# First norm, first chunk and last norm of a two-layer hybrid decoder trunk

## The reference

```python
def rmsnorm(x, g):
    y = xf * lax.rsqrt(jnp.mean(xf * xf, axis=-1, keepdims=True) + EPS)
    return y * g
for l in range(DEPTH):
    x = x + 0.5 * swiglu_ffn(rmsnorm(x, norm_ffn1[l]), w_ffn1_in[l], w_ffn1_out[l])
    u = rmsnorm(x, norm_mix[l]); proj = u @ w_in[l]
    ...  # retention, pooling and convolution branches, gated and merged
    x = x + merged @ w_out[l]
    x = x + 0.5 * swiglu_ffn(rmsnorm(x, norm_ffn2[l]), w_ffn2_in[l], w_ffn2_out[l])
return rmsnorm(x, norm_final)
```

## Time and profile before

| | us |
|---|---|
| median of 3 runs | 1225.2 (1223.81 to 1225.21) |
| the profiled execution: its own time | 1225.4 |
| the profiled execution: span in the trace | 1223.6 |
| PE busy in the span | 1176.9 (96%) |
| DVE busy | 755.6 (62%) |
| ACT busy | 533.9 (44%) |
| POOL busy | 56.6 (5%) |
| mean granted clock of PE, share of full | 0.988 |

### The profile page before, as it was taken

One profiled execution on the slowest core, in us unless ns is written; L12 is line 12 of the kernel. 1 busy time (PEld: TensorE's weight loads), 2 busy tenths in 40 slices (PEclk: granted clock), 3 DMA queues, 4 the chain that ended last, 5 costly groups with the idle time before them and its releaser, 6 DMA issues.

```text
span 1223.6 us, 13278 instructions
## 1 busy us (share of the span) xinstructions
PE 1176.9 (96%) x5360; PEld 969.5 (79%) x5360; DVE 755.6 (62%) x903; ACT 533.9 (44%) x586; POOL 56.6 (5%) x73
## 2 busy tenths in 40 slices
PE   6999999999988999999999999999999699999997
PEld 5888887888866878888878888878887587888886
DVE  5554465796798664554465545467959977645442
ACT  7444345443434454443364444354433255444331
POOL 3000001000000010000020000020000001000000
PEclk9999999999988999999999999999999899999999
DMA  8655364553643455445554545545346344644440
GB/s 331 241 202 189 123 243 167 207 180 111 225 155 137 143 202 184 165 167 206 206 209 170 207 149 211 192 170 206 121 143 253 121 157 153 224 175 170 171 172 35
DMA packets 33661, 220.02 MB, mean 180 GB/s; under 512 B 3760, under 2 KB 4144, under 8 KB 8640
## 3 DMA queue, kind: packets, MB, share of 16 engines
q1 hardware_dynamic: 31104, 212.09, 47.4%
q0 software_dynamic: 1648, 6.06, 1.4%
q10 hardware_dynamic: 848, 1.02, 0.2%
HBM read 218.10 MB, written 1.05 MB: 179 GB/s over the span
## 4 chain that ended last, share of the span: by engine, by line
PE 86%; DVE 10%; ACT 2%; DMA 1%; issue 1%; SPq 0%; DVEq 0%; POOL 0%; POOLq 0%; ACTq 0%
PE acc L302 27%; PE acc L304 27%; PE acc L303 27%; DVE w_lo L884 4%; DVE y L1064 4%; PE tr L360 4%; DMA raw<-in_weights 1%; ACT w_hi L599 1%; DVE xT_lo L918 1%; ACT xT_hi L611 0%; DVE gates L1132 0%; DVE ua L1113 0%; DVE x L898 0%; PE tr L451 0%; PE tr L461 0%
## 5 line engine op out<-in xcount | busy, mean ns | idle before, releaser
L884 DVE TENSOR_TENSOR w_lo<-raw,w_hi 128x2048 fp32r<-128x2048 f32 (+2 forms) x207 | 451.1, 2212 | 108.4 <-ACT w_hi L599 107.8
L599 ACT CAST w_hi<-raw 128x2048 fp32r<-128x2048 f32 (+2 forms) x207 | 380.2, 1850 | 254.8 <-PE acc L304 252.9
L302 PE MATMUL acc<-w_hi,xT_hi 128*128 128x512 f32 x1184 | 475.8, 402 | 13.3 <-DVE gates L1132 6.3
L304 PE MATMUL acc<-w_hi,xT_lo 128*128 128x512 f32 x1184 | 465.6, 393 | 0.0
L303 PE MATMUL acc<-w_lo,xT_hi 128*128 128x512 f32 x1184 | 464.9, 393 | 0.0
L302 PEld LDWEIGHTS acc<-w_hi,xT_hi 128*128 128x128 f32 x1184 | 225.0, 190 | 59.6 <-DVE gates L1132 7.1
L304 PEld LDWEIGHTS acc<-w_hi,xT_lo 128*128 128x128 f32 x1184 | 224.4, 190 | 48.8
L303 PEld LDWEIGHTS acc<-w_lo,xT_hi 128*128 128x128 f32 x1184 | 224.9, 190 | 43.6
L937 DVE SCALAR_TENSOR_TENSOR h<-acc,rs,silu_gate 128x256 f32<-128x256 f32 x88 | 42.5, 483 | 223.0 <-ACT silu_gate L643 223.0
L302 PE MATMUL acc<-w_hi,hT_hi 128*128 128x512 f32 x352 | 137.9, 392 | 0.0
L304 PE MATMUL acc<-w_hi,hT_lo 128*128 128x512 f32 x352 | 137.1, 389 | 0.0
(11 more groups left out here) (104 smaller groups left out, 556.1 us busy)
## 6 DMA issues: line engine op xcount, KB each, us to landing
raw<-in_weights SPq DMA_DIRECT2D x195, 1024.0 KB, 4.8
raw<-in_weights SPq DMA_DIRECT2D x8, 512.0 KB, 3.4
bias<-in_gate_bias POOLq DMA_DIRECT2D x6, 512.0 KB, 7.7
raw<-in_weights SPq DMA_DIRECT2D x8, 256.0 KB, 3.6
scale_row<-in_pool_scale POOLq DMA_DIRECT2D x2, 512.0 KB, 9.1
out<-x SPq DMA_DIRECT2D x4, 256.0 KB, 2.1
x<-in_x ACTq DMA_DIRECT2D x3, 256.0 KB, 7.6
band<-in_band POOLq DMA_DIRECT2D x1, 768.0 KB, 8.8
```

Source lines behind the costliest of these rows:

```text
L302: nc.tensor.matmul(o, a_hi, b_hi, start=first, stop=False)
L304: return nc.tensor.matmul(o, a_lo, b_hi, start=False, stop=last)
L599: nc.scalar.copy(w_hi[:, hf % HIGHS, 0:n], raw[:, hf % RAWS, 0:n]).then_inc(hi_split, 1)
L884: nc.vector.tensor_tensor(w_lo[:, hf % RAWS, 0:n], raw[:, hf % RAWS, 0:n], w_hi[:, hf % HIGHS, 0:n].bitcast(F32), ALU.subtract).then_inc(l ...
```

## The change

- The array `ident` gets 8 more columns that hold the gains of the first norm; `x_high` and `x_low` of the first norm read their scale there, and ACT and DVE wait for `ident_landed` in place of `par_landed`. The load of `par` is issued after the two quarters of x for t = 1, and is waited for at the end of the first FFN.
- Before and between PE's first transposes, 7, 2 and 6 matmuls of zeros run (`keep_busy`), on a row that DVE sets at the start (`warm_set`). They write to a bank of PSUM (`ret`) that nobody reads then.
- `cast_first` and `sub_first` now go over eight eighths of chunk 0: half 1 is cast and subtracted in four quarters too (its load is one DMA as before), and PE waits at each k for its eighth.
- `x_high` and `x_low` of t = 1 come right behind the eighths. The squares of t = 0, `cast(2)` and `cast(3)` come behind `x_high` of t = 1, and `sub(2)` behind `x_low` of t = 1.
- The end: the squares are made by halves (n = 0, 1), POOL adds eps to the first, adds the second, and takes the power (two instructions behind the last squares); DVE multiplies each half by the gain as soon as it is added (`weighted`); behind the root, ACT scales and stores half 0, DVE scales and SP stores half 1.
- POOL's load of `scale_row` of layer 0 waits for the first product.

```diff
-        ident = sb("ident", [P, P])
+        ident_gain = sb("ident_gain", [P, P + KT])
+        ident = ident_gain[:, 0:P]
...
-                    if t == 0 and hf == 0:
+                    if t == 0 and hf < 2 and k < KT - 1:
                         pe.wait_ge(first_lo, k + 1)
+                    elif t == 0 and hf == 1:
+                        pe.wait_ge(lo_split, 1)
...
+            def keep_busy(n):
+                warm = scale_row[:].bitcast(BF16)
+                for _ in range(n):
+                    nc.tensor.matmul(ret[:, 0, :], warm[:, 0:P], warm[:, 0:NB], start=True, stop=True)
+            pe.wait_ge(warm_set, 1)
+            keep_busy(7)
             pe.wait_ge(ident_landed, 16)
             turn_x(0, 0, 0, 0)
+            keep_busy(2)
             turn_x(0, 0, 0, 1)
+            keep_busy(6)
...
-            act.dma_start(par[:], params.rearrange("l p n -> p l n")).then_inc(par_landed, 16)
             for c in (0, 1):
                 act.dma_start(x[:, 1, columns(c)], x_part(1, c)).then_inc(x_landed[1][c], 16)
+            act.dma_start(par[:], params.rearrange("l p n -> p l n")).then_inc(par_landed, 16)
...
             def cast_first(i):
-                act.wait_ge(first_landed[i], 16)
-                nc.scalar.copy(w_hi[:, 0, columns(i)], raw[:, 0, columns(i)]).then_inc(first_hi, 1)
+                hf, s = i // 4, columns(i % 4)
+                if i < 4:
+                    act.wait_ge(first_landed[i], 16)
+                elif i == 4:
+                    act.wait_ge(raw_landed[1], 16)
+                nc.scalar.copy(w_hi[:, hf, s], raw[:, hf, s]
+                               ).then_inc(first_hi if i < 7 else hi_split, 1)
...
                 x_high(l, norm, 1, 0)
                 x_high(l, norm, 1, 1)
+                if l == 0 and norm == 0:
+                    square(l, norm, 0)
+                    for hf in (2, 3):
+                        cast(hf)
                 cast(l * HALVES + 2 * g + 4)
...
-            act.wait_ge(par_landed, 16)
+            act.wait_ge(ident_landed, 16)
             x_high(0, 0, 0, 0)
             cast_first(0)
+            cast_first(1)
             x_high(0, 0, 0, 1)
-            for i in range(1, 4):
+            for i in range(2, 8):
                 cast_first(i)
-            cast(1)
-            square(0, 0, 0)
-            cast(2)
-            cast(3)
...
+            for t in range(T):
+                for n in (0, 1):
+                    wait_acc_taken(act, L - 1, FFN2 + FB, t, n)
+                    nc.scalar.activation(squares[:, columns(n)], x[:, t, columns(n)], ACT.Square,
+                                         scale=D ** -0.5, accum_out=end_meansq[:, t, n:n + 1]
+                                         ).then_inc(end_meansq_ready, 1)
+                act.wait_ge(end_rs_ready, t + 1)
+                act.wait_ge(end_weighted, 2 * t + 1)
+                nc.scalar.activation(weighted[:, t, columns(0)], weighted[:, t, columns(0)],
+                                     ACT.Copy, scale=end_rs[:, t:t + 1]).then_inc(out_ready[0], 1)
+                act.wait_ge(out_ready[0], t + 1)
+                act.dma_start(out.rearrange("a (t p) d -> p (a t) d", p=P)[:, t, columns(0)],
+                              weighted[:, t, columns(0)]).then_inc(stored, 16)
...
+            nc.vector.memset(scale_row[:, 0:NB // 2], 0.0).then_inc(warm_set, 1)
...
             for t in range(T):
                 for n in (0, 1):
                     add_next(L, 0, t, n)
-            dve.wait_ge(bias_landed, 48 * L + 16)
-            for t in range(T):
-                dve.wait_ge(rs_ready, 6 * L + t + 1)
-                for n in (0, 1):
                     wait_acc_taken(dve, L - 1, FFN2 + FB, t, n)
-                    nc.vector.scalar_tensor_tensor(x[:, t, columns(n)], x[:, t, columns(n)],
-                                                   rs[:, t:t + 1], bias[:, columns(n)],
-                                                   ALU.mult, ALU.mult).then_inc(out_ready, 1)
+                    nc.vector.tensor_tensor(weighted[:, t, columns(n)], x[:, t, columns(n)],
+                                            bias[:, columns(n)], ALU.mult
+                                            ).then_inc(end_weighted, 1)
+                dve.wait_ge(end_weighted, 2 * t + 2)
+                dve.wait_ge(end_rs_ready, t + 1)
+                nc.vector.tensor_scalar(weighted[:, t, columns(1)], weighted[:, t, columns(1)],
+                                        end_rs[:, t:t + 1], None, ALU.mult
+                                        ).then_inc(out_ready[1], 1)
```

More of the change, by code:

```diff
@@ L177, in trunk @@
         rot = st
+        weighted = gates
         ysilu = v
@@ L233, in trunk @@
         setup_act = sem("setup_act")
-        out_ready = sem("out_ready")
+        warm_set = sem("warm_set")
+        end_meansq_ready = sem("end_meansq_ready")
+        end_eps_added = sem("end_eps_added")
+        end_totalled = sem("end_totalled")
+        end_rs_ready = sem("end_rs_ready")
+        end_weighted = sem("end_weighted")
+        out_ready = [sem(f"out_ready{n}") for n in (0, 1)]
         PRODUCT = {}
@@ L243, in trunk, with gain @@
         uses = [[0, 0] for _ in range(T)]
+        def gain(l, norm, k):
+            if l == 0 and norm == 0:
+                return ident_gain[:, P + k:P + k + 1]
+            return par[:, l, PAR_GAIN[norm] + k:PAR_GAIN[norm] + k + 1]
         def tokens(t):
@@ L609, in x_high @@
                     k = 4 * c + i
-                    col = PAR_GAIN[norm] + k
                     nc.scalar.activation(xT_hi[:, k, tokens(t)],
                                          bank(("x", l, norm, t, c))[:, i * P:(i + 1) * P],
-                                         ACT.Copy, scale=par[:, l, col:col + 1]
+                                         ACT.Copy, scale=gain(l, norm, k)
                                          ).then_inc(x_hi_ready, 1)
@@ L888, in sub_first @@
             def sub_first(i):
[L889 to L892, removed]
+                hf, s = i // 4, columns(i % 4)
+                if i < 7:
+                    dve.wait_ge(first_hi, i + 1)
+                else:
+                    dve.wait_ge(hi_split, 1)
+                nc.vector.tensor_tensor(w_lo[:, hf, s], raw[:, hf, s], w_hi[:, hf, s].bitcast(F32),
+                                        ALU.subtract).then_inc(first_lo if i < 7 else lo_split, 1)
             def add_x(l, g, use, t, n, half):
@@ L916, in x_low @@
                     k = 4 * c + i
-                    col = PAR_GAIN[norm] + k
                     a = nc.vector.scalar_tensor_tensor(
                         xT_lo[:, k, tokens(t)], bank(name)[:, i * P:(i + 1) * P],
-                        par[:, l, col:col + 1], xT_hi[:, k, tokens(t)].bitcast(F32),
+                        gain(l, norm, k), xT_hi[:, k, tokens(t)].bitcast(F32),
                         ALU.mult, ALU.subtract)
@@ L961, in ffn @@
                         begin(l, 3 * f)
+                        if l == f == 0:
+                            sub(2)
                     else:
@@ L1289, in mixer @@
                 finish(l, 3, l * HALVES + 2 * (M_OUT + 1) + 4)
-            dve.wait_ge(par_landed, 16)
+            dve.wait_ge(ident_landed, 16)
             x_low(0, 0, 0, 0)
             sub_first(0)
+            sub_first(1)
             x_low(0, 0, 0, 1)
-            for i in range(1, 4):
+            for i in range(2, 8):
                 sub_first(i)
-            sub(1)
-            sub(2)
             for l in range(L):
@@ L1387, in _ @@
                            ).then_inc(bias_landed, 16)
-            norm_factor(L, 0)
+            for t in range(T):
+                s = slice(t, t + 1)
+                pool.wait_ge(end_meansq_ready, 2 * t + 1)
+                nc.gpsimd.tensor_tensor(end_eps[:, s], end_meansq[:, t, 0:1], small[:, 1:2],
+                                        ALU.add).then_inc(end_eps_added, 1)
+                pool.wait_ge(end_eps_added, t + 1)
+                pool.wait_ge(end_meansq_ready, 2 * t + 2)
+                nc.gpsimd.tensor_tensor(end_total[:, s], end_meansq[:, t, 1:2], end_eps[:, s],
+                                        ALU.add).then_inc(end_totalled, 1)
+                pool.wait_ge(end_totalled, t + 1)
+                nc.gpsimd.tensor_tensor(end_rs[:, s], end_total[:, s], small[:, 0:1],
+                                        ALU.pow).then_inc(end_rs_ready, 1)
 def decay_table():
```

28 lines of the change are left out of this document (19 added, 9 removed).

## The result

| | median, us | runs | ratio to before, 95% interval |
|---|---|---|---|
| before | 1224.75 | 4 (1223.81 to 1225.21) | |
| changed | 1239.54 | 4 (1238.88 to 1240.61) | 1.0122, 1.0109 to 1.0134 |

The changed kernel is 14.8 us slower; the forecast was 1221.4, faster. (The median before is of four executions here, of three where it stood at 1225.2.) The profiled execution took 1238.9 us with a span of 1236.7.

What follows compares the result with a forecast made beforehand. PE, working 96% of the span, was taken as the bound, with gains only at the two ends: 1225.4 - 2.7 (start) - 1.1 (end) = 1221.6, forecast 1221.4 because the profiled execution lies 0.2 us above the median; range 1219.0 to 1223.3.

Steps and rivals of the forecast that it cites:

- rival D: Rings and hidden values move some tens of bytes; if reads slow, all 5360 matmuls pay: 1232 us at 2 ns; chance 0.03.
- Gains with the identity: Start: ACT can begin before 8.45 us; by itself no gain, since ACT waits for half 1 until 13.13.
- Products of zeros: Start of PE: seven end at 4.2 us, first transposes slip from 3.88 to 4.2, first product at 8.4 instead of 11.52.
- Rival B: Products of zeros fail, PE at 1.2 GHz through all of t = 0: gain 2.6 us, 1222.6; chance 0.12.
- rival A: Clock doesn't fall in the wait before k = 4: gain 4.0 + 1.1 = 5.1 us, 1220.1; chance 0.30.
- Eighths: Half 1 in four quarters at the start: costs ACT 0.5 us more, but PE gets k = 4 at 14.5 us.
- the order: ACT at the start: `x_high` of t = 1 starts at 15.4 us instead of 19.75; PE could start t = 1 at 17.8.
- when t = 1 starts: PE ends t = 0 at 17.6 us, about when ACT's chain is ready: start at 17.8 instead of 22.19, gain 4.4.
- The fall of the clock behind the wait: PE's 2 us wait for k = 4 drops the clock, costing 1.7 us (bounds 0 and 1.7); start gain becomes 2.7.
- `turn_h`: First hidden block's transposes: PE there at 28.8 us, waiting 0.2 to 0.8, with a high clock; 30.5 with it fallen.
- The end: Behind PE's last matmul: 1.5 us saved, less 0.4 for stores starting together; gain 1.1 us, bounds 0.7 and 1.5.

Runs made afterwards that it cites:

- the rings at 70016: The changed kernel with the start of the weight rings and all behind them moved on by 96 bytes (from 69920): 1219.18 us, ratio to before 0.9961.

## Why the prediction was wrong

**The direction: rival D.** The prediction named the mechanism, the place and the threshold (1.2 ns a matmul), and gave it 0.03. Measured are 6.3 ns on 3744 of the matmuls. The step that failed is its one argument against: that 0.23 us a matmul was found alike for operands in rings and in fixed tiles. That is so, but in the kernel before all of these have the same remainder of distance, 0 (the table above), so no row of it could show what another remainder costs. The sum of the forecast has the move at nothing for this reason alone. I took a trace in which a thing never varied as evidence that it doesn't matter. What would have helped is to add up the sizes of the tiles between xT and the rings; it shows that the move is 160 bytes, not the "some tens" of the prediction, and no multiple of a power of two above 32. Why the chip pays for the distance no run shows.

The Trainium skill has the rule of where an operand may start ("SBUF — State Buffer", section "Operand start alignment") and says that it is about legality, that the runs behind it timed nothing. All of the kernels here obey it; it says nothing for or against this cost.

**The size.** D was priced at 10.7 us for 2 ns on all 5360; at 6.3 ns on 3744 it is 23.6, of which 20.4 arrive; PE runs into DVE's convolution later and waits less there.

**The parts, by the prediction's steps.**

1. Gains with the identity "by itself gives nothing": doubtful. Taking them back costs some 0.5 us in the trace and 1.6 between the medians, which isn't clear of noise. The step looked at the wait for half 1 alone and not at the transposes of t = 1, which stand in PE's order between the products.
2. Products of zeros: the times were right to 0.1 us (first transposes 4.16, forecast 4.2; first product 8.46, forecast 8.4), their worth is nothing that the runs can tell. Rival B had their failure at 1222.6, 2.5 us above rival A, with a low clock through all of t = 0; the clock rises near 11 us even without them.
3. Eighths, 4. the order, and 5. when t = 1 starts: `x_high` of t = 1 at 15.25 (forecast 15.4), k = 4 at 14.56 (14.5), t = 1 at 17.90 without a wait (17.8). Right.
6. The fall of the clock behind the wait: it didn't come. The waits for k = 4 were 1.82 us in the changed kernel, 1.6 with the rings aligned and 1.2 without the zeros, and the clock stayed high behind each; the 2.25 us wait of rows 6 was not near enough to go by. Rival A held.
7. `turn_h` at 29.15, forecast 29.2 for rival A, but not by its mechanism: the second `hidden(0, ...)` ended at 28.94 and PE, slowed by its matmuls, came at 29.15 without a wait. With the rings at 70016 it is as forecast: PE is through at 28.3 and waits until 28.59. POOL's first instruction for t = 1 again lay behind DVE's subtraction (2.03 us for 0.19).
8. The end: 6.2 us from the last addition in place of 7.05, -0.85 against a forecast of -1.1 (0.7 to 1.5). ACT's multiplication takes 0.72 (forecast 0.6), its store 2.6 us where SP's, issued 0.17 us ahead of it, takes 2.1. The rule of the Trainium skill that two issuing engines bring no bandwidth ("DMA: Bandwidth & Descriptors", section "Rules for kernel authors") would have cost 0.8 us by the prediction's estimate; the trace agrees with its direction, with 0.5 us more on one of the two stores. That 0.3 to 0.4 us appear outside the span was not foreseen.

With the distance put right, the kernel is at 1219.2 us, 5.4 below before. Rival A had 5.1 (1220.1), and the stated forecast 3.8. That the 5.1 fits so well is in part luck: in the trace with the rings at 70016 the start gained 4.6 in place of 4.0, with half 1 landing 0.4 us sooner than before, and the end gave 0.3 in the medians in place of 1.1. The time of the changed kernel was decided by a thing that stands in no line of the schedule.

## What to carry to other kernels

A diff that only adds a few bytes to a tile moves all that is allocated behind it: write down the addresses of both operands of the commonest matmul before and after, and for fp32r operands like these keep their distance a multiple of 256 bytes; here 96 bytes of padding are worth 20.4 us in 1240. A wait that is made longer by an early start costs twice, since the clock may fall in it: move what ends the wait together with what starts it. When a row is used as evidence that something doesn't matter, ask whether that thing varies in the trace.

## What the runs showed of the hardware

- A matmul of 512 fp32r columns with a 128 x 128 fp32r stationary operand takes 227 to 228 ns from start to start when the two operands' distance in the partition is a multiple of 256 bytes (remainder 0), 229.1 with 64, and 232.9 to 234.1 with 32, 96, 128, 160, 192 and 224. It follows the distance, not the place (both moved by 32: 227.7). Only fp32r operands were tried, and which of the two reads is held up, the load of the weights or the stream, was not shown: the mean of the load in the records is 190 ns either way.
- PE's clock stayed at 2.4 GHz behind waits of 1.2, 1.6 and 1.8 us at the start; of two waits of 2.25 and 2.27 us (rows 6) it was at 1.2 GHz behind the first alone; and in a wait of 4.29 us it fell, for 6.8 us in all.
- Half 1 of the weights landed 1.4 us apart in two executions of kernels with the same start (ACT began on it at 12.70 and at 14.11), and the first hidden block was turned 1.4 us apart too (28.59 and 30.00).
- Two stores of 256 KB issued 0.17 us apart on two queues took 2.1 and 2.6 us, and kernels that end so have 2.1 to 2.3 us outside their span in place of 1.8 to 1.9.
